# A two-layer four-mixer decoder trunk on eight cores: 64-query score blocks with the mask folded into the contraction, tanh gates, placed table loads, and a reordered beginning and end

## The reference

```python
xn = rmsnorm(x, norm_mix[l])
proj = xn @ w_in[l]
z_a, z_b, q, k, v, z_d, z_g = jnp.split(proj, PROJ_SPLITS, axis=-1)
y_a = spatial_gating(jax.nn.gelu(z_a, approximate=False), ...)   # 128x128 position matrices in chunks
y_b = conformer_conv(z_b, ...)        # GLU a*sigmoid(gate), depthwise conv of width 31, layernorm, silu
q = rotary(q.reshape(b, s, N_Q_HEADS, HEAD_DIM), cos, sin)       # 8 query heads of 64
k = rotary(k.reshape(b, s, N_KV_HEADS, HEAD_DIM), cos, sin)      # 2 key heads of 64
y_c = sliding_window_attention(q, k, v, attn_sinks[l])           # window 128, one sink logit per head
y_d = short_gated_conv(z_d, sc_w[l])
branch = jnp.einsum('nbsc,ncd->nbsd', ys, w_branch[l])
gates = jax.nn.sigmoid(z_g.reshape(b, s, N_BRANCH, D_MODEL))
x = x + jnp.einsum('bsnd,nbsd->bsd', gates, branch) @ w_out[l]
gate, up = jnp.split(rmsnorm(x, norm_ffn[l]) @ w_gate_up[l], 2, axis=-1)
x = x + (jax.nn.silu(gate) * up) @ w_down[l]
```

## Time and profile before

| | |
|---|---|
| median of 3 runs (lowest, highest) | 2532.87 us (2530.97, 2533.39) |
| profiled execution: its own time | 2530.34 us |
| its span, core 4 | 2529.3 us |
| spans of the 8 cores | 2520.4 to 2529.3 us |
| mean granted TensorE clock | 0.990 to 0.994 of full |
| PE (TensorE) busy | 2464.3 us, 97% |
| DVE, ACT, POOL busy | 1427.2, 1185.1, 450.2 us |

### The profile page before, as it was taken

One profiled execution on the slowest core, in us unless ns is written; L12 is line 12 of the kernel. 1 busy time (PEld: TensorE's weight loads), 2 busy tenths in 40 slices (PEclk: granted clock), 3 DMA queues, 4 the chain that ended last, 5 costly groups with the idle time before them and its releaser, 6 DMA issues.

```text
span 2529.3 us, 35812 instructions; the slowest of 8 cores (2520.4 to 2529.3 us)
## 1 busy us (share of the span) xinstructions
PE 2464.3 (97%) x12322; PEld 1127.8 (45%) x12322; DVE 1427.2 (56%) x2244; ACT 1185.1 (47%) x1970; POOL 450.2 (18%) x488
## 2 busy tenths in 40 slices
PE   5999999999999999999999999999999899999998
PEld 1444444444444444444444444444444344444443
DVE  4167443799647543599927544379955664433112
ACT  2165984411126797422106699541114669823111
POOL 0041234000004223200003223400000322330000
PEclk8999999999999999999999999999999999999999
DMA  7122247533552336734364225743336323373433
GB/s 158 34 51 51 51 101 164 99 71 73 114 121 51 54 60 130 160 74 81 61 150 85 50 51 108 169 91 74 67 69 134 71 51 63 70 156 67 79 58 90
DMA packets 48769, 221.97 MB, mean 88 GB/s; under 512 B 4688, under 2 KB 4944, under 8 KB 37840
## 3 DMA queue, kind: packets, MB, share of 16 engines
q0 software_dynamic: 26496, 163.59, 36.7%
q1 hardware_dynamic: 22096, 56.10, 6.9%
HBM read 366.47 MB, written 16.78 MB: 152 GB/s over the span
## 4 chain that ended last, share of the span: by engine, by line
PE 92%; DMA 3%; ACT 2%; DVE 2%; issue 1%; POOL 0%; SPq 0%; DVEq 0%; ACTq 0%; POOLq 0%
PE psum L782 91%; DMA arena<-x 2%; PE psum L786 1%; DVE arena L850 1%; DMA y<-arena 1%; ACT arena L816 1%; ACT L816 1%; DMA arena<-rope 1%; DVE arena L843 0%; DVE arena L833 0%; ACT arena L822 0%; POOL arena L833 0%; SPq L868 0%; DVEq L156 0%; DVE arena L1050 0%
## 5 line engine op out<-in xcount | busy, mean ns | idle before, releaser
L782 PE MATMUL psum<-arena 128*128 128x512 bf16 (+4 forms) x11826 | 2441.5, 364 | 51.2 <-ACT arena L816 23.5
L782 PEld LDWEIGHTS psum<-arena 128*128 128x128 bf16 (+2 forms) x11826 | 1099.0, 98 | 1373.6 <-issue 129.9
L833 DVE TENSOR_TENSOR arena<-psum,arena 128x512 f32<-128x512 f32 (+1 forms) x576 | 387.5, 687 | 553.8 <-PE psum L782 306.2
L850 DVE SCALAR_TENSOR_TENSOR arena<-arena 128x1024 f32<-128x1024 bf16 (+3 forms) x648 | 615.7, 991 | 53.5 <-ACT arena L816 44.9
L816 ACT ACTIVATE arena<-psum 128x512 bf16<-128x512 f32 (+1 forms) x536 | 311.3, 597 | 655.3 <-PE psum L782 653.2
L816 ACT ACT_TABLE_LOAD x318 | 408.0, 1283 | 64.2 <-PE psum L782 44.2
L833 POOL TENSOR_TENSOR arena<-arena 128x512 bf16<-128x512 f32 (+1 forms) x264 | 329.8, 1256 | 439.6 <-DVE arena L833 403.6
L816 ACT ACTIVATE arena<-arena 128x512 bf16<-128x512 f32 (+3 forms) x356 | 194.7, 576 | 278.9 <-DVE arena L833 236.8
L833 DVE TENSOR_TENSOR arena<-arena,psum 128x512 f32<-128x512 f32 (+1 forms) x160 | 109.0, 686 | 275.3 <-PE psum L782 273.5
L822 ACT COPY arena<-psum 128x1024 bf16<-128x1024 bf16 (+2 forms) x96 | 81.5, 849 | 180.0 <-PE psum L782 122.6
L816 ACT ACTIVATE arena<-psum,arena 128x256 bf16<-128x256 f32 (+3 forms) x284 | 138.4, 489 | 57.4 <-PE psum L782 54.0
(11 more groups left out here) (17 smaller groups left out, 161.4 us busy)
## 6 DMA issues: line engine op xcount, KB each, us to landing
arena<-wgu POOLq DMA_DIRECT2D x44, 1024.0 KB, 8.8
arena<-win POOLq DMA_DIRECT2D x48, 768.0 KB, 7.5
arena<-win POOLq DMA_DIRECT2D x28, 1024.0 KB, 10.5
arena<-wdn POOLq DMA_DIRECT2D x32, 704.0 KB, 6.6
arena<-x SPq DMA_DIRECT2D x24, 512.0 KB, 9.5
arena<-wbr POOLq DMA_DIRECT2D x16, 768.0 KB, 9.8
arena<-wout POOLq DMA_DIRECT2D x8, 1024.0 KB, 13.5
xmid<-arena SPq DMA_DIRECT2D x16, 512.0 KB, 8.9
```

The source lines that it names most:

```text
L782: return ((lambda: nc.tensor.matmul(o.ap, lhsT=l.ap, rhs=r.ap, start=start, stop=stop)), [l, r], [o])
L833: vec(eng, o, nel(a), lambda: eo.tensor_tensor(out=o.ap, in0=a.ap, in1=b.ap, op=op), [a, b], shift=shift)
L850: vec("dve", o, nel(a), lambda: nc.vector.scalar_tensor_tensor(out=o.ap, in0=a.ap, scalar=(sc.ap if isinstance(sc, Ref) else sc), in1=b.ap ...
```

## The change

**Scores.** A block of 128 queries becomes two sub-blocks of 64. The stationary operand is 64 queries of two heads (128 columns), the moving operand 192 keys (three runs of 64). The contraction has 128 rows: 64 of them are q and k channels, the other 64 are a one-hot row per query (`hotb`) against a band of 0 and -30000 (`bandb`), so that the mask comes out of the same matmul. Four matmuls of 192 columns take the place of eight of 256. For this, `fills` writes the one-hot and band patterns into `qa` and `KA` (buffers that lie over `XN` of the other half and over the old `qT`, `yglu`, `cacc` region) once per half, and `q_unit` and `k_unit` copy the rotated q and k into them on DVE (`put_k` writes each key block three times). The keys of the half before are kept in `khist`. The probabilities lie in tiles that are zero outside the band (32 small memsets on POOL), so `att_b` and `att_c` keep their eight 128-column matmuls each, with the heads in another order.

**Gates.** sigmoid(z) is written as (1 + tanh(z/2))/2: ACT computes Tanh into f32, DVE a scalar_tensor_tensor `(s + 1) * p` instead of a product; the factor 0.5 goes into the convolution's last activation and into `wout_unit`. Tanh is in the tables of Exp, Gelu and Silu.

**Table loads** are now instructions in the program, put where the planner switches. The program has 76.

**Beginning and end.** The first convolution weights come in two pieces; the second input block is loaded only after them; three of the four diagonal matrices are built after the first norm; `glu_unit` and `conv_pe` run for channels 0, 1 and then 2, 3; `conv_pe` is split into pieces of 8 matmuls. In the last half the second token block of the last four `down_unit`s, the last norm and its stores are split into pieces of 256 columns.

**Planner.** A DMA no longer holds back the look-ahead, the assumed transfer rate falls from 250e3 to 225e3, the buffer arena grows from 206000 to 212832 bytes, and a DMA's completion no longer stands for the engine work issued before it.

```diff
-            sc = bank((1024,))
-            parts = []
-            pr = slice(hh * 64, hh * 64 + 64)
-            for g in range(4):
-                parts.append(mmp(sc[:, g * nk:(g + 1) * nk], qT[pr, g, n * 128:(n + 1) * 128], kT[pr, k0:k0 + nk], True, False))
-                parts.append(mmp(sc[:, g * nk:(g + 1) * nk], identb.all(), amb[:, 256 - nk:256], False, True))
-            pe(parts, [nk] * 8, reserve=2)
...
+            for e in range(2):
+                i, nk = n * 2 + e, nks[e]
+                nr = nk // 64
+                sc = bank((2, nk))
+                scs.append(sc)
+                k0 = i * 192 + (3 - nr) * 256
+                kv = ka[hh][:, k0:k0 + nr * 256].re(lambda a, nr=nr: a.rearrange("p (r c) -> p r c", r=nr)[:, :, 0:64])
+                pe([mmp(sc[:, p, :], qa[hh][:, p, i, :, :].re(lambda a: a.rearrange("p g t -> p (g t)")), kv, True, True) for p in range(2)],
+                   [nk] * 2, reserve=1)
+                vec("dve", A(2 * e, 2 * e + 2), 2 * nk, lambda e=e, sc=sc: nc.vector.tensor_reduce(
+                    out=A(2 * e, 2 * e + 2).ap, in_=sc.all().ap, axis=AX.X, op=ALU.max), [sc.all()])
...
+        def fills():
+
+            for r in range(2):
+                o = qa[r].all().re(lambda a: a.rearrange("p a b g t -> p (a b g) t"))
+                i = hotb.all().re(lambda a: a.rearrange("p (b t) -> p b t", b=1).to_broadcast([128, 64, 64]))
+                vec("dve", o, 4096, lambda o=o, i=i: nc.vector.tensor_copy(out=o.ap, in_=i.ap), [i], 2.0)
+                o = ka[r].all().re(lambda a: a.rearrange("p (b t) -> p b t", b=19))
+                i = bandb.all().re(lambda a: a.rearrange("p (b t) -> p b t", b=1).to_broadcast([128, 19, 192]))
+                vec("dve", o, 3648, lambda o=o, i=i: nc.vector.tensor_copy(out=o.ap, in_=i.ap), [i], 2.0)
...
+        def put_k(src, b0, nb):
+
+            for r in range(2):
+                rows = slice(r * 64, r * 64 + 64)
+                o = ka[r][rows, b0 * 192:(b0 + nb) * 192].re(lambda a: a.rearrange("p (b r t) -> p b r t", r=3, t=64))
+                i = Ref(src.tile, rows, src.fk, lambda a: a.rearrange("p (b r t) -> p b r t", r=1, t=64).to_broadcast([64, nb, 3, 64]))
+                vec("dve", o, nb * 192, lambda o=o, i=i: nc.vector.tensor_copy(out=o.ap, in_=i.ap), [i], 2.0)
...
         def q_unit(j, b):
-            rope(w3(W["q"], 0, 8, 512), j, b, qT[:, j, b * NB:(b + 1) * NB])
+            qt = bft()
+            rope(w3(W["q"], 0, 8, 512), j, b, qt.all())
+            for k in range(2):
+                rows = slice(k * 64, k * 64 + 64)
+                cp("dve", qa[k][rows, j // 2, b * 8:(b + 1) * 8, j % 2, :], qt[rows].re(lambda a: a.rearrange("p (b t) -> p b t", t=64)))
...
-            s = bft()
-            act(s.all(), pg.all(), AF.Sigmoid)
+            s = f32t()
+            act(s.all(), pg.all(), AF.Tanh, scale=0.5)
...
-                    tt(m.all(), pb.all(), s.all(), ALU.mult)
+                    stt(m.all(), s.all(), 1.0, pb.all(), ALU.add, ALU.mult)
...
-            unit(n0 - (0.5 if H or b == 0 else 16), ld)
+            unit(n0 - (0.5 if H or b == 0 else 45.2), ld)
...
                 if H == 0 and b == 1:
-                    rd = [xs[:, 6:8, :]]
+                    rd = [W0["cf0"].all()]
...
-                unit(T["qkv"] + (-62, -14, 0, 7)[c], lambda c=c: diag_unit(c))
+                unit(T["qkv"] + (-62, -14.8, 14, 21)[c], lambda c=c: diag_unit(c))
...
+        if t.load is not None:
+            P.add("act", (lambda t=t: nc.scalar.preload_act_table_set(t.load)))
```

More of the change, by code:

```diff
@@ L373 @@
 class Task:
-    __slots__ = ("eng", "parts", "cost", "occ", "prio", "when", "idx", "npred", "succ", "tiles", "table", "dma", "nbytes",
+    __slots__ = ("eng", "parts", "cost", "occ", "prio", "when", "idx", "npred", "succ", "tiles", "table", "load", "dma", "nbytes",
                  "reserve", "start", "end")
@@ L397, in add @@
         t.table = table
+        t.load = None
         t.dma = dma
@@ L466, in can @@
         def can(t):
-            while done[front[0]]:
+            while front[0] + 1 < len(done) and (done[front[0]] or self.tasks[front[0]].dma is not None):
                 front[0] += 1
@@ L496, in pick @@
                 sc = c[0]
-                if e == "act" and t.table is not None and t.table != table[0] and not (t.table == "exp" and table[0] == "ln"):
+                if e == "act" and t.table is not None and table[0] not in t.table:
                     sc += table_slack
@@ L525, in run @@
                     extra = 0.0
-                    if e == "act" and t.table is not None and t.table != table[0] and not (t.table == "exp" and table[0] == "ln"):
-                        table[0] = t.table
+                    if e == "act" and t.table is not None and table[0] not in t.table:
+                        table[0] = t.load = t.table[0]
                         extra = table_cost
@@ L753, in build_program @@
     xs = fixed([8, NB], F32, XS0)
-    qT = fixed([4, HT], BF16, XS0)
+    qa = [fixed([2, 16, 2, 64], BF16, XS0 + r * 8192) for r in range(2)]
+    KA = [[fixed([3648], BF16, XN[i].off + r * 7296) for r in range(2)] for i in range(2)]
     xs0 = fixed([8, NB], F32, R1)
@@ L963, in norm1_unit @@
         return load, go
+    W0 = {}
     def half(H, T):
@@ L971, in half, with wl_parts @@
         t0 = h * HT
-        W = {}
+        W = W0 if H == 0 else {}
         def wl(name, src, n, after=()):
             W[name] = load_w(src, n, after)
+        def wl_parts(name, src, n, after):
+            t = W[name] = Tile([n], BF16, pool=p_w)
+            for i in range(2):
+                cs = slice(i * n // 2, (i + 1) * n // 2)
+                dma("pool", t[:, cs], src[:, cs], list(after), [t[:, cs]], "%s%d" % (name, i), 64 * n * 4, shift=-60.0)
         def win(g):
@@ L1146, in conv_dve @@
                 if k == 0:
-                    ts(ac.all(), yglu[:, c, 0:HT], wc(0), ALU.mult, sm[:, SM_CVB + c:SM_CVB + c + 1], ALU.add, rate=1.0)
+                    ts(ac.all(), yglu[:, c, 0:HT], wc(0), ALU.mult, rate=1.5)
                 else:
@@ L1424, in build_program @@
         fn()
-    order = PL.run(dma_rate=250e3, dma_lat=2.0, table_cost=1.3, table_slack=12.0, ahead=40.0)
+    order = PL.run(dma_rate=225e3, dma_lat=2.0, table_cost=1.3, table_slack=12.0, ahead=40.0)
     print("planned span:", PL.span)
```

208 lines of the change are left out of this document (121 added, 87 removed).

## The result

The changed kernel takes 2443.27 us, the median of four runs, beside 2533.13 us of the kernel before on the same chip. The ratio is 0.964, with a 95% interval of 0.962 to 0.966. The forecast was 2434 us and a ratio of 0.961. The profiled execution took 2442.41 us, its span on core 2 is 2441.4, and the other cores' spans run from 2431.3 on, at granted clocks of 0.992 to 0.997.

A forecast was written before the change was run, and what follows sets the result against it. PE was taken as the bound, working 2464.3 of 2529.3 us. Terms -81.5 (PE), -10.5, -6, +2, -3 sum to -99: 2431.3 profiled, 2434 us median, ratio 0.961; own range 2418 to 2448, whole range 2412 to 2468.

The forecast's parts named there:

- the beginning: Before PE's unbroken run: lost time falls from 37.2 to 26.7 us, -10.5 us (bounds 0 and -15).
- H = 3: Last half's start, where PE waits 8.9 us behind stores, rotary tables and DVE: chain unchanged, more DVE work, +2 us.
- the end: After the last matmul: eight products of 512 columns become 256 and halve, steps before them shrink, -3 us.
- The scores: 60 full score blocks on PE: 1.65 us each becomes 0.33, together 99 to 20 us, -79.
- The four lone blocks: Score blocks at the head of a sequence: eight matmuls of 128 become four small ones, -5 us.
- The rival of short matmuls staying slow: Score matmuls on PE: 0.2 us belongs to scores as such, not the alternation; +28 us, 2462; chance 0.09.
- The products with V: Attention products on PE: output half now changes at each instruction, +2 us taken (bounds -16 and +4).
- Gates and tables: ACT sheds 242 table loads, 310 us, already hidden behind PE; only short stalls come back, -6 us (0 to -16).
- The copies: New DVE copies: 13 us a half, 52 in all; hidden for the first three halves.
- The rival with slow copies: DVE copies at one element a cycle: 19 instead of 8 us a half in q and k; +25, 2459; chance 0.10.
- Its sign: For slow copies: PE's waits name DVE copies at q and k.
- the slower case: DVE becomes the bound from q and k into attention, all copies on PE's path: +44 us, 2577; chance 0.02.

The follow-up runs named there:

- experiments 1 and 2: The kernel before, with mask matmuls contracting over 64 rows (1: ratio 0.988) or score matmuls over all 128 rows (2: ratio 0.984).
- experiment 6: The changed kernel with the old beginning (weights, second x block, diagonal products, GLU and convolution order), convolution still in pieces of 8: 2449.2 us, ratio 0.967.
- experiment 3: The changed kernel with sigmoid gates again, with a table set of their own: 2444.65 us, ratio 0.967.
- experiment 4: The changed kernel with the 64 query copies (64 rows by 512, bf16) on ACT instead of DVE: 2422.1 us, ratio 0.956.

## Why the prediction was off by 9 us, step by step

The span fell by 87.9 us (2529.3 to 2441.4), against 99 in the sum. The rows divide it so: PE's busy time outside the beginning -82.5 (87.0 less 9.0 - 4.5), the beginning -12.5, H = 3 -1.9, the end -1.6, other idle time +10.6 (from 16.2 to 26.8).

**The scores: right.** -79 was forecast; 60 x (1.71 - 0.33) = 83 by the matmuls' starts. (The prediction's 1.78 is a little high because it took 0.2139 us for a matmul of 512: 187 in 40 us counts those cut off at both ends; their starts lie 0.2158 apart.) The four lone blocks fell from 1.28 to 0.17 us where nothing else holds them up, 4.4 in all, forecast 5. The reading that the busy share hid a slow block, and that alternation was its cause, is borne out by experiments 1 and 2. The rival of short matmuls staying slow is out: 0.083 us each, not 0.2. The Trainium skill, page "TensorEngine Tiling (Array Packing)", section "Key Properties", says that a change of tiling mode drains TensorE; the runs don't show a drain as such, but they agree that a change between 64 and 128 rows costs time, 0.105 us each.

**The products with V: nothing.** +2 was taken; eight push the next start back by 0.45 us in either kernel. Changing the half at each instruction instead of at every second costs nothing.

**The beginning: right in sum (-12.5 against -10.5), half right in cause.** The norm's products no longer stand behind the diagonal ones (18.32 instead of 24.19 us), and two diagonal products hold the GLU product to 32.23 us, as forecast. But what ends PE's waits is the weights (21.51) and the second x block (3.14 us, where 2 were allowed), not the GLU product. 5.2 us come from something that the working didn't see at all, most likely ACT's order (experiment 6).

**Gates and tables: -6 forecast, nothing measured.** The loads are 76 as planned. With 168 the time was 2.2 us longer, within what the runs differ by, and PE's waits for ACT were the same (experiment 3). The argument that these 310 us were hidden holds as far as it was tried, and the 6 us taken in spite of it don't show.

**The copies: the step that failed.** "The rest, 8 us a half, falls into q and k, where it is busy 26.99 of 40, so 13 us are free", and so "Hidden for H = 0 to 2". Both halves of it failed. The query and key copies take 13.9 us a half ((43.0 + 12.6) / 4), since the price came from the mean of a tensor_scalar that rarely meets POOL, and was used for copies that mostly do. The trace of the kernel before had the effect in it: of its 240 tensor_scalars of 256 elements, 26 ran into a POOL instruction and took 0.84 us, the other 214 took 0.28. And the copies weren't free to take even the room there was: rotary products that free PE's banks wait in DVE's queue behind them, as at 745.82 us. Moving the query copies alone gives back 20 us (experiment 4), 11 as idle time and 9 as busy time, 18 of them in H = 0 to 2, where the copies were to be hidden. The rival with slow copies had this mechanism with +25 us, by another cause of slowness. Its sign, that PE's waits name DVE copies, didn't show, because PE waits for the products behind them. (Two of the prediction's terms here don't follow from its own figures: 29824 elements at 1.08 ns are 32 us a half, not 36, so the slower case would have been +30 us and not +44, and by 0.27 us fixed and 0.27 ns an element the 24 instructions of a half take 14.5 us, not 13.)

**H = 3 and the end** were mis-sized a little. For H = 3 +2 was forecast and -1.9 came: the same chain, a little shorter. Of the end's -3 only 1.6 came, since the third quarter's eight products moved ahead of the last residual addition; I had read only the last matmul's own tail.

Worked out again: -83 - 4.4 + 0.5 on PE, -12.5, -1.9, -1.6, and +20 for the copies come to -82.9, 5 us short of the measured -87.9. But experiment 4 took 14 us off PE's idle time outside the beginning, H = 3's wait and the end (26.8 to 12.8), and only 10.6 of that had come with the change (16.2 before). By that share some 15 of its 20 us are the copies' cost (an estimate), and the sum is -87.9; that it fits to the tenth is chance.

The total was also lucky. The copies (+15), the gates (+6) and the end (+1.4) came out worse than forecast, the scores (-4), H = 3 (-3.9), the beginning (-2) and the V products (-2) better, so about half of the first errors was cancelled by the second.

## What to carry to other kernels

Divide an engine's busy time by what its plain instructions cost before calling the engine the bound: here 0.84 of the 1.71 us a block were neither columns nor waits. Price work that is moved onto a second engine with the neighbours it will have there, for DVE with what POOL does at that moment, and look at its place in the queue and not at the free share of a stretch. Taking stalls out of TensorE was worth about twice their length in experiment 4 (20.3 us of span for 10.9 of idle time), where the clock had fallen behind them.

## What was not expected of the hardware

- A bf16 copy of 64x512 on DVE takes 0.284 us with POOL at rest and 0.671 in the mean beside POOL's additions; one of 64x1536 takes 0.551 and 0.785.
- Score matmuls of 256 columns whose rows alternate between 64 and 128 cost 0.21 us each, all with 128 rows 0.11; each change costs 0.105 us.
- Taking out stalls of 10.9 us shortened the busy time of the same matmuls by 9.4 (experiment 4), with the granted clock of one stretch at 1.00 instead of 0.91.
- An activation starts right behind a table load: in the kernel before a load begins at 36.39 us, takes 1.28, and the activation begins at 37.68. All 318 loads of that trace are followed 0.012 us later.
